# Rows of the residual taken while the last norm is made, experts' rows scaled by ScalarE and GpSimd, shared down product by tokens

## What is computed

```python
h = rms_norm(x, g)                       # norm_ffn
eidx, gw = route(h, w_r, bias)           # sigmoid scores, best 4 of 8 groups, best 8 of 64 experts
y = routed_experts(h, eidx, gw, w_gate, w_up, w_down)
y = y + (jax.nn.silu(h @ s_gate) * (h @ s_up)) @ s_down      # the shared expert
x = x + y                                # and a last rms_norm gives the output
```

## Time and profile before

| | |
|---|---|
| median of 3 runs | 1110.92 us (1109.17 to 1112.01) |
| profiled execution | 1109.17 us, span of its instructions 1107.4 us |
| TensorE busy | 1061.4 us (96%), mean granted clock 0.982 of 2.4 GHz |
| VectorE busy | 748.3 us (68%) |
| ScalarE busy | 646.5 us (58%) |
| GpSimd busy | 262.8 us (24%) |

### The profile page before, as it was taken

The page is one execution under the profiler, slowest core; times in us unless marked ns, Lnnn a source line. Parts: engine busy times, 40 slices in busy tenths (PEclk is TensorE's granted clock), DMA queues, the critical chain, the costliest instruction groups (busy, mean ns, idle before and its releaser), DMA issues.

```text
span 1107.4 us, 17623 instructions
## 1 busy us (share of the span) xinstructions
PE 1061.4 (96%) x5991; PEld 796.5 (72%) x5991; DVE 748.3 (68%) x1332; ACT 646.5 (58%) x850; POOL 262.8 (24%) x180
## 2 busy tenths in 40 slices
PE   5999999999999999999999999999999999999991
PEld 5999458999669888666667666766667666766660
DVE  4733834633934575787788777887788778887762
ACT  4374343432643313677767776677767776677662
POOL 1001320000000101233333333333333333333321
PEclk8999999999999899999999999999999999999996
DMA  9500336050953525899999999999999999999945
GB/s 300 225 4 31 142 143 229 1 229 27 379 211 157 227 79 192 288 359 375 368 367 369 368 377 363 351 357 357 364 366 369 359 356 358 369 367 374 361 113 172
DMA packets 64342, 299.02 MB, mean 270 GB/s; under 512 B 12591, under 2 KB 15227, under 8 KB 39718
## 3 DMA queue, kind: packets, MB, share of 16 engines
q1 hardware_dynamic: 49102, 261.93, 61.7%
q0 software_dynamic: 15200, 36.55, 13.4%
HBM read 281.34 MB, written 34.00 MB: 285 GB/s over the span
## 4 chain that ended last, share of the span: by engine, by line
PE 90%; DMA 3%; DVE 3%; ACT 2%; SPq 1%; issue 1%; POOLq 0%; ACTq 0%; DVEq 0%
PE pair L1920 23%; PE pair L181 18%; PE pair L1954 16%; PE pair L1933 10%; PE pair L1659 5%; PE pair L1905 5%; PE pair L1562 3%; PE pair L1940 1%; DMA regA<-in_w_in 1%; PE pS L1868 1%; PE pair L1752 1%; PE pair L1760 1%; PE pS L1731 1%; DMA acc_rows<-regL 1%; DMA regL<-h_rows,regL 1%; DVE regL L1113 1%
## 5 line engine op out<-in xcount | busy, mean ns | idle before, releaser
L1920 PE MATMUL pair<-w_hi,h_parts 128*96 128x512 f32 x768 | 267.7, 430 | 0.0
L715 POOL DMA_INDIRECT acc_rows<-regL x64 | 93.0, 1453 | 389.8 <-ACT regL L1032 275.2
L1920 PEld LDWEIGHTS pair<-w_hi,h_parts 128*96 128x96 f32 x768 | 121.5, 165 | 69.7 <-issue 33.9
L1954 PE MATMUL pair<-w_hi,act_parts 128*96 128x512 f32 x512 | 165.0, 404 | 2.6 <-DVE act_parts L1509 2.6
L706 POOL DMA_INDIRECT regL<-h_rows,regL x65 | 139.7, 2148 | 74.7 <-DVE regL L1351 49.4
L1032 ACT ACTIVATE regL<-pair,regL 96x1024 f32<-96x1024 f32 x64 | 71.1, 1110 | 125.0 <-PE pair L1954 125.0
L1455 DVE TENSOR_TENSOR lo_A<-regA,w_hi 128x1536 fp32r<-128x1536 f32 x64 | 111.9, 1749 | 0.2 <-ACT w_hi L992 0.2
L1954 PEld LDWEIGHTS pair<-w_hi,act_parts 128*96 128x96 f32 x512 | 80.2, 167 | 29.9 <-issue 2.8
L992 ACT CAST w_hi<-regA 128x1536 fp32r<-128x1536 f32 x64 | 94.7, 1482 | 0.0
L1505 DVE TENSOR_TENSOR lo_B<-regB,w_hi 128x2048 fp32r<-128x2048 f32 x32 | 73.4, 2293 | 29.6 <-ACT w_hi L1027 29.6
L1505 DVE TENSOR_TENSOR lo_A<-regA,w_hi 128x2048 fp32r<-128x2048 f32 x32 | 73.4, 2292 | 24.7 <-ACT w_hi L1027 24.7
(11 more groups left out here) (344 smaller groups left out, 2207.3 us busy)
## 6 DMA issues: line engine op xcount, KB each, us to landing
regA<-in_exp_w_gate SPq DMA_DIRECT2D x32, 1024.0 KB, 9.1
regA<-in_exp_w_up SPq DMA_DIRECT2D x32, 1024.0 KB, 12.2
regA<-in_exp_w_down SPq DMA_DIRECT2D x32, 1024.0 KB, 14.0
regB<-in_exp_w_down SPq DMA_DIRECT2D x32, 1024.0 KB, 15.3
regB<-in_exp_w_gate SPq DMA_DIRECT2D x16, 1024.0 KB, 10.0
regB<-in_exp_w_up SPq DMA_DIRECT2D x16, 1024.0 KB, 13.6
regC<-in_exp_w_gate SPq DMA_DIRECT2D x16, 1024.0 KB, 9.2
regC<-in_exp_w_up SPq DMA_DIRECT2D x16, 1024.0 KB, 12.6
```

The costliest lines, as they stand in the source:

```text
L715: pool.indirect_dma_start(acc_rows, bass.IndirectOffsetOnAxis(ap=kept[0:SLOTS, r, 0:1].bitcast(U32), axis=0), yX[r][0:SLOTS, :], None, bou ...
L1920: ins = pe.matmul(out, x, w, start=False, stop=half == 1 and k == CUT_K - 1 and s == 2, skip_group_check=True)
L1954: ins = pe.matmul(pair[2][0:SLOTS, h, :], act_parts[:, x, k, :], w[:, k, cols], start=k == 0 and s == 0, stop=k == KF - 1 and s == 2)
```

## The change

The rows are now made from the residual `xT` instead of from the normed `hT`: the products "xr" replace "hR" and "sr". TensorE transposes tile 0 between the two parts of `sum_squares`, tiles 1 and 2 ahead of the spread, tile 3 ahead of the router's product, tile 4 behind it. VectorE copies tile 0 out, ScalarE the others, into `rows`. ScalarE then scales each row by `rs` into five new places `hrow` (two of them are where the first gathers land, two where expert 1's down weights go), GpSimd multiplies these by the gain, which a DMA early in the kernel spreads over all partitions (`gain_all`), and SP sends them to `h_rows`. Expert 1's down weights are loaded behind that. The shared down product is made token tile by token tile: the activations are stationary and the weights stream in 512 columns; VectorE adds it to `rows`, and GpSimd's queue sends these to `acc_rows` as the additions are done.

```diff
-    o += [(("x2", m), "dve") for m in range(KD)] + [("nb3", "dve")]
-    o += [("rt", "act"), (("hR", 0), "dve"), ("rs", "act")]
-    o += [(("hR", t), "act") for t in range(1, NTT)]
+    o += [(("x2", m), "dve") for m in range(KD)]
+    o += [(("xr", 0), "dve"), (("xr", 1), "act"), (("xr", 2), "act"), ("nb3", "dve"), (("xr", 3), "act")]
+    o += [("rt", "act"), (("xr", 4), "act"), ("rs", "act")]
...
-    o += [(("sd", m), "dve", 2, (m + 1) % 3) for m in range(KD)]
-    o += [(("sr", t), "act", 2, 2 - 2 * (t % 2)) for t in range(NTT)]
+    o += [(("sd", t), "dve", 2, (t + 1) % 3) for t in range(NTT)]
...
+        hrow = [view(regL, 8824, D), view(regL, 9848, D), view(regA, 10240, D), view(regA, 11264, D), view(regL, 12952, D)]
...
+            sp.dma_start(gain_all[:, :], norm_ffn.rearrange("o d -> (o d)").partition_broadcast(P)).then_inc(gain_in, 16)
             sp.dma_start(wk_v, xa_wk.rearrange("o (k p) n -> p (o k) n", p=P)).then_inc(wk_in, 16)
...
             for t, (t0, n) in enumerate(TILES):
-                J.wait_taken(sp, ("hR", t))
-                sp.dma_start(h_rows[t0:t0 + n, :], rows[0:n, t, :]).then_inc(h_stored, 16)
-
+                sp.wait_ge(h_rows_made, t + 1)
+                sp.dma_start(h_rows[t0:t0 + n, :], hrow[t][0:n, :]).then_inc(h_stored, 16)
+            sp.wait_ge(h_stored, 16 * NTT)
+            sp.dma_start(WD[1][:, :, :], ed[1:2].rearrange("e p k d -> p (e k) d")).then_inc(wd_in[1], 16)
...
+            pool.wait_ge(gain_in, 16)
+            for t, (t0, n) in enumerate(TILES):
+                pool.wait_ge(h_scaled, t + 1)
+                pool.tensor_tensor(hrow[t][0:n, :], hrow[t][0:n, :], gain_all[0:n, :], ALU.mult).then_inc(h_rows_made, 1)
+
             pool.wait_ge(row_table, 1)
...
-                J.wait_taken(pool, ("sr", t))
+                J.wait_taken(pool, ("sd", t))
                 pool.dma_start(acc_rows[t0:t0 + n, :], rows[0:n, t, :]).then_inc(sums_landed, 16)
...
+            J.wait_taken(a, ("xr", 0))
+            J.wait_taken(a, ("xr", TT))
+            a.wait_ge(consts, 17)
+            for t, (t0, n) in enumerate(TILES):
+                a.activation(hrow[t][0:n, :], rows[0:n, t, :], ACT.Copy, scale=rs[0:n, t:t + 1]).then_inc(h_scaled, 1)
...
             residual("x2", 2 * KP + KD)
+            p = J.wait_made(v, ("xr", 0))
+            J.take(v.tensor_copy(rows[:, 0, :].rearrange("p (h n) -> p h n", h=2), pair[p][:, :, :]), ("xr", 0))
             inverted()
...
+            def shared_added(t):
+                n = TILES[t][1]
+                p = J.wait_made(v, ("sd", t))
+                J.take(v.tensor_tensor(rows[0:n, t, :].rearrange("p (h n) -> p h n", h=2),
+                                       rows[0:n, t, :].rearrange("p (h n) -> p h n", h=2), pair[p][0:n, :, :], ALU.add), ("sd", t))
...
+            squares_of("x2", lambda: residual_rows(0))
+            residual_rows(1)
+            residual_rows(2)
             spread("nb3")
+            residual_rows(3)
...
-            rows_of(("hR", 0), hT, *TILES[0])
+            residual_rows(TT)
...
+                            for i, (x, w) in enumerate(((0, sdw_hi), (1, sdw_hi), (0, sdw_lo))):
+                                ins = pe.matmul(pair[p][0:n, h, :], shared_parts[:, x, kf, t0:t0 + n], w[:, kf, cols],
                                                 start=kf == 0 and i == 0, stop=kf == KF - 1 and i == 2)
...
             turn(0, 0, 0, first=True)
-            for t, (t0, n) in enumerate(TILES):
-                rows_of(("sr", t), xT, t0, n)
-            J.wait_taken(pe, ("sr", 3))
+            J.wait_taken(pe, ("sd", 2))
```

More of the change, by code:

```diff
@@ L591, in _ @@
             sp.dma_start(WG[e][:, 1:2, :], eu[e:e + 1].rearrange("e p n -> p e n")).then_inc(wg_in[e], 16)
-            sp.wait_ge(made, J.no[("sd", KD - 1)] + 1)
+            sp.wait_ge(made, J.no[("sd", NTT - 1)] + 1)
             sp.dma_start(WD[e][:, :, :], ed[e:e + 1].rearrange("e p k d -> p (e k) d")).then_inc(wd_in[e], 16)
@@ L961, in _, with take_rows @@
             rooted(D)
+            def take_rows(t):
+                n = TILES[t][1]
+                p = J.wait_made(a, ("xr", t))
+                J.take(a.copy(rows[0:n, t, :].rearrange("p (h n) -> p h n", h=2), pair[p][0:n, :, :]), ("xr", t))
+            for t in (1, 2, 3):
+                take_rows(t)
             a.wait_ge(sh_in, 48)
@@ L968, in _ @@
             J.take(a.activation(sT[NE:2 * NE, :], pair[p][NE:2 * NE, 0, 0:QUARTER + DEC], ACT.Sigmoid), "rt")
[L970 to L973, removed]
+            take_rows(TT)
             p = J.wait_made(a, "rs")
@@ L995, in _ @@
                 cut_up(0, 0, 0, half)
-            a.wait_ge(h_stored, 16 * NTT)
-            def start_sums(t):
-                n = TILES[t][1]
-                p = J.wait_made(a, ("sr", t))
-                J.take(a.copy(rows[0:n, t, :].rearrange("p (h n) -> p h n", h=2), pair[p][0:n, :, :]), ("sr", t))
             a.wait_ge(row_table, 1)
@@ L1035, in _ @@
             turn(0)
-            for t in range(NTT):
-                start_sums(t)
             def step_of_block(i, j, peeled=False):
@@ L1351, in slots @@
                 v.tensor_scalar(sums[0:SLOTS, r, 0:1].bitcast(U32), sums[0:SLOTS, r, 0:1], float(FAR), None, ALU.add).then_inc(idx_ready, 1)
-            p = J.wait_made(v, ("hR", 0))
-            J.take(v.tensor_copy(rows[:, 0, :].rearrange("p (h n) -> p h n", h=2), pair[p][:, :, :]), ("hR", 0))
             J.wait_taken(v, "rs")
@@ L1699, in into_residual, with squares_of @@
                     product(m)
-                if what == "x2":
-                    squares_of(what)
-            def squares_of(what):
+            def squares_of(what, between=None):
                 added = KD - 2 if what == "x1" else 2 * (KD - 2)
@@ L1708, in squares_of @@
                 seen["squares"] += KD - 1
+                if between:
+                    between()
                 sum_squares(at, sq, False, True)
@@ L1813, in _, with rows_of, residual_rows @@
             into_residual("x2", lambda m: X.product(pe, pair, m, o_hi, o_lo, out_split if m == 0 else None, half_first=m == 0))
+            def rows_of(name, src, t0, n):
+                p = J.begin(pe, name)
+                for k in range(KD):
+                    ins = pe.transpose(pair[p][0:n, k // 4, (k % 4) * P:(k % 4 + 1) * P], src[:, k, t0:t0 + n], ident[:, :])
+                J.made_by(ins)
+            def residual_rows(t):
+                if t == 0:
+                    J.wait_taken(pe, ("x2", KD - 1))
+                rows_of(("xr", t), xT, *TILES[t])
+            squares_of("x2", lambda: residual_rows(0))
+            residual_rows(1)
+            residual_rows(2)
             spread("nb3")
+            residual_rows(3)
             ready = normed_tiles(0, "nb3", KD)
@@ L1824, in _ @@
             J.made_by(ins)
-            def rows_of(name, src, t0, n):
-                p = J.begin(pe, name)
-                for k in range(KD):
-                    ins = pe.transpose(pair[p][0:n, k // 4, (k % 4) * P:(k % 4 + 1) * P], src[:, k, t0:t0 + n], ident[:, :])
-                J.made_by(ins)
-            rows_of(("hR", 0), hT, *TILES[0])
+            residual_rows(TT)
             p = J.begin(pe, "rs")
@@ L1892, in _ @@
             slots(1)
-            for m in range(2, KD):
-                shared_down(m)
-            J.wait_taken(pe, ("sd", 6))
+            for t in range(2, NTT):
+                shared_down(t)
+            J.wait_taken(pe, ("sd", 3))
             def turn(g, b, q, first=False):
```

41 lines of the change are left out of this document (16 added, 25 removed).

## The result

The changed kernel takes 1118.97 us (median of 7 runs), the kernel before 1110.92 (7 runs beside them): 0.8% slower, ratio 1.0081, 95% interval 1.0061 to 1.0101. Forecast were 1114.5 us and a range up to 1117.4. The direction was right, the size too small by more than the range allowed. The profiled execution took 1117.91 us, so it is 8.74 us longer than the one before (1109.17).

The account below looks back on a forecast made before the run. TensorE, busy 96% of the span, was taken as the bound. +5.55 + 1.5 - 2.6 - 0.85 = +3.6 us gave 1112.8 on the profiled 1109.17, 1114.5 on the median; range 1105.5 to 1117.4.

Parts of the forecast that it names:

- Clock ahead of the router: Transposes added in TensorE's waits before the router's scores make these end 1.9 us later, at 385.3 us.
- the rival with chance 0.20: Transposes fill TensorE's holes at 371 to 380 and keep its clock up: 2 us less, 1112.5; chance 0.20.
- GpSimd's duration and the hold: In VectorE's routing: GpSimd's gain multiplications take 2.3 us each and hold VectorE's two-input operations, delaying the chosen experts 7.0 us.
- Start of "pos": TensorE's slot counts, which wait for the chosen experts, start at 408.15 us, 5.55 us later than before.
- Low clock behind the pause: After TensorE's idle time ahead of the slot counts, 1.2 GHz loses 0 to 2.5 us; +1.5 taken.
- Shared down product by tokens: From the up products' end to the first expert product: 17.1 us instead of 19.7, so -2.6 us.
- Third gather: In the expert loop, TensorE's wait for gathered rows ahead of the third block's transposes goes: -0.85 us.
- Whatever moves its start moves the end by as much: The expert loop is not touched, so any shift of its start shifts the kernel's end equally.
- the rest up to the third turn: From the shared up products' end to the third block's transposes of gathered rows: -2.6 and -0.85 us.

Follow-up runs that it names:

- The 16 products in the pause: Changed kernel plus 16 unused 128x260 products on TensorE ahead of its wait for the chosen experts; 1112.36 us, ratio 1.0020.
- behind it (1.9 us of loss): Changed kernel plus 16 unused 128x260 products on TensorE right after its wait for the chosen experts; 1122.91 us, two runs.
- both edits: Changed kernel with experts' rows made on VectorE and GpSimd where VectorE waits, and third gather issued ahead of the wait for sums; 1108.08 us, ratio 0.9983.
- the 2 us: Kernel with both edits plus 16 unused transposes on TensorE ahead of the third block's transposes; 1105.55 us, ratio 0.9956.

## Why the prediction was wrong, and what of it was right

*Clock ahead of the router: the step was wrong, a rival right.* The forecast left 1.9 us in because no row showed transposes alone keeping the clock up; that they do was the rival with chance 0.20. The router ended 0.1 us later by its own doing, not 1.9, and routing started at 386.19, not 387.9. In three of 17 profiles the clock fell here all the same and the router ended 1.7 us later, so the forecast was right for a minority of executions.

*GpSimd's duration and the hold: right.* 2.3 us forecast, 2.33 measured; hold 7.0 forecast, 7.0 measured; one operation of VectorE gets in behind each of GpSimd's, as the four rows of the old trace had suggested. That the size came out to a tenth is partly luck: the steps were forecast 2.5 us apart, which made 7.5, and a guessed 0.5 was taken off for a second operation slipping in. None slipped in; the steps were 2.3 us apart, because GpSimd's operations followed each other without a gap. What the Trainium skill (SBUF — State Buffer, Who interferes with whom) says of copies and casts in VectorE's two-port modes agrees with this trace: the cast of 40 columns took 0.94 us instead of 0.18 and ended at 392.07 with GpSimd's second operation. Maxima and index searches beside GpSimd were not held (40 maxima in 2.81 us both times).

*Start of "pos": near.* +5.55 forecast, +3.97 measured: the 1.9 us of the clock did not come, and 0.3 us had been lost ahead of any edit.

*Low clock behind the pause: the term that failed.* The prediction put it: "Last time the low clock lasted 5 us into the products ... at up to half speed that loses 0 to 2.5 us. I take +1.5." It lost 6.5 us. The pause and its clock were foreseen; wrong was the bound, which took the 5 us of another place, where large products ran, for a property of the clock. Here "pos" ran first and it lasted 13 us from its start. The 16 products in the pause (no loss) and behind it (1.9 us of loss) show that what runs after the pause sets the length. This term alone carries the time out of the range: with 1.5 in its place the profile would stand at 1112.9, where 1112.8 was forecast. That agreement is luck: "pos" started 1.6 us sooner than forecast, and 1.8 us less were won behind the up products; the two errors cancel.

*Shared down product by tokens: right.* First expert product 17.3 us behind the up products, forecast 17.1.

*Third gather: wrong in the changed kernel.* The forecast had its 0.85 us of wait gone; it grew to 1.59. The sums left GpSimd's queue as forecast (+17.0 us), but the last took 5.73 us to land, not 4.4, and the gather behind it 9.46, not 8.5, which is not explained (chain of waits):

```profile
448.66 5.73 DMA acc_rows<-regL
...
455.31 9.46 DMA regL<-h_rows,regL
```

So from the up products on 1.64 us were won instead of 3.45.

*"Whatever moves its start moves the end by as much": wrong as a rule.* It held for the first profile (loop 0.6 us longer up to the last turn, the end 0.1 us sooner), but where the loads' landing times climbed to 28 us the loop added up to 5 us, in the changed kernel's second profile too.

The sum, forecast and measured in the profile: start of "pos" +5.55 and +3.97, low clock +1.5 and +6.50, the rest up to the third turn -3.45 and -1.64, from there to the end 0 and -0.09: +3.6 and +8.74.

## What to carry to other kernels

Cost a pause of TensorE by what runs after it: the same 7.3 us pause lost 1.9 us ahead of 260-column products, 5.4 to 6.5 ahead of the 64-column ones of "pos", and nothing when filled with useless products. Elementwise work moved to GpSimd is not free while VectorE runs a chain of short two-input operations: five operations of 2.3 us cost that chain 7 us, and the same work in VectorE's own pauses cost nothing. Before counting a microsecond won ahead of a loop, look at how long its loads take to land and whether that time is stable; here the loop took gains of up to 3.5 us back some 400 us later, when TensorE began to wait for its loads.

## What of the hardware was not expected

- With 32 transposes of 128x128 in TensorE's short waits the granted clock stayed at 1.00 in 14 of 17 profiles, where it had fallen to 0.50 in the one without them, so that 3.9 us of added work cost 0.1. In the other three it fell, and they cost 1.7.
- The low clock outlasted 8.6 us in which TensorE had no pause (40 matmuls of 64 columns), and 2.2 to 4.4 us of larger ones behind them, in all four profiles.
- Cutting GpSimd's operations in two halved each of VectorE's waits (2.3 to 1.2 us) and left their sum as it was (routing 20.2 us both times).
- A load of 1 MB landed in 9 us or in 28 us in the same stretch of the loop (880 to 960 us, both edits with and without the 2 us), at 374 and 362 GB/s in all.
